# Layer norms of a two-block network: mean, squares, high parts and first tiles rearranged

## The reference

```python
def second_block(x, w_in, conv_w, w_out, ln1_g, ln1_b, w_up, ffn_conv_w, w_down, ln2_g, ln2_b, rel_bias):
    for l in range(DEPTH):                                       # DEPTH = 2
        mix = hybrid_mixer(x, w_in[l], conv_w[l], w_out[l], rel_bias)
        x = layer_norm(DN_ALPHA * x + mix, ln1_g[l], ln1_b[l])   # "norm", l, 0
        f = conv_ffn(x, w_up[l], ffn_conv_w[l], w_down[l])
        x = layer_norm(DN_ALPHA * x + f, ln2_g[l], ln2_b[l])     # "norm", l, 1
    return x

def layer_norm(x, g, b):
    mu = jnp.mean(x, axis=-1, keepdims=True)
    var = jnp.mean(jnp.square(x - mu), axis=-1, keepdims=True)
    return (x - mu) * lax.rsqrt(var + LN_EPS) * g + b

def conv_ffn(h, w_up, ffn_conv_w, w_down):
    u = h @ w_up                                  # 1024 -> 2 x 2816
    a, b = u[..., :D_FF], u[..., D_FF:]
    a = causal_dwconv(a, ffn_conv_w)              # 3 taps
    return (gelu(a) * b) @ w_down                 # 2816 -> 1024
```

## Time and profile before

| | us |
|---|---|
| median of 3 runs | 2670.54 (2667.34 to 2671.54) |
| the profiled execution | 2673.33 |
| its span (first to last instruction) | 2671.5 |
| PE busy | 2513.2 (94%) |
| DVE busy | 1814.5 (68%) |
| ACT busy | 1312.6 (49%) |
| POOL busy | 29.6 (1%) |
| chain that ended last | PE 83%, DVE 9%, ACT 6% |

### The profile page before, as it was taken

How to read it: one execution, slowest core, us unless ns; L and a number is a source line. 1 busy time by engine, 2 the same in 40 slices (tenths; PEclk the granted TensorE clock), 3 DMA queues, 4 the chain that set the end, 5 groups by cost and what they waited for, 6 DMA issues and landing times.

```text
span 2671.5 us, 33651 instructions
## 1 busy us (share of the span) xinstructions
PE 2513.2 (94%) x13358; PEld 2053.7 (77%) x13358; DVE 1814.5 (68%) x2870; ACT 1312.6 (49%) x1981; POOL 29.6 (1%) x29
## 2 busy tenths in 40 slices
PE   6999998999998989899999999999898999998998
PEld 3464657788776658688788887888798899988998
DVE  4778626676431434699899898898867675576774
ACT  2135513222222343577677776787644554444553
POOL 0000000000000000000000000000000000000000
PEclk8999998999998989899999999999999899998999
DMA  7522023555321102498898897898843345432552
GB/s 287 189 109 96 1 79 111 189 203 190 125 79 48 64 32 80 184 353 340 309 366 325 324 368 292 325 366 328 310 143 125 111 174 201 146 128 109 176 188 95
DMA packets 71675, 512.06 MB, mean 192 GB/s; under 512 B 7904, under 2 KB 9056, under 8 KB 10048
## 3 DMA queue, kind: packets, MB, share of 16 engines
q1 hardware_dynamic: 68688, 500.20, 50.2%
q10 hardware_dynamic: 2208, 7.37, 0.7%
q0 software_dynamic: 592, 1.97, 0.2%
HBM read 507.27 MB, written 2.23 MB: 191 GB/s over the span
## 4 chain that ended last, share of the span: by engine, by line
PE 83%; DVE 9%; ACT 6%; issue 1%; DMA 1%; DVEq 0%; ACTq 0%
PE bank L767 81%; DVE UL L1892 1%; ACT UH L1433 1%; DVE arena L1900 1%; DVE arena L1892 1%; ACT arena L1436 1%; ACT HT L1436 1%; DMA XT<-in_x 1%; PE bank L1076 1%; DVE HGl L1892 1%; DVE HT L1892 1%; ACT L1436 1%; DVE JUNK L1939 0%; DVE arena L1896 0%; DVE small L1959 0%
## 5 line engine op out<-in xcount | busy, mean ns | idle before, releaser
L1892 DVE TENSOR_TENSOR UL<-ring,UH 128x1024 fp32r<-128x1024 f32 x738 | 886.0, 1212 | 213.6 <-ACT UH L1433 194.3
L1433 ACT CAST UH<-ring 128x1024 fp32r<-128x1024 f32 x738 | 761.4, 1039 | 352.7 <-PE bank L767 344.5
L767 PE MATMUL bank<-XH,UH 128*128 128x256 f32 x1040 | 308.9, 297 | 9.6 <-DVE XL L1892 8.3
L767 PE MATMUL bank<-UH,HGh 128*128 128x512 f32 (+1 forms) x768 | 292.8, 381 | 17.9 <-DVE HT L1892 6.6
L767 PE MATMUL bank<-XL,UH 128*128 128x256 f32 x1040 | 297.6, 286 | 0.0
L767 PE MATMUL bank<-XH,UL 128*128 128x256 f32 x1040 | 297.3, 286 | 0.0
L767 PE MATMUL bank<-UH,HGl 128*128 128x512 f32 (+1 forms) x768 | 289.9, 377 | 0.0
L767 PE MATMUL bank<-UL,HGh 128*128 128x512 f32 (+1 forms) x768 | 288.9, 376 | 0.0
L1433 ACT CAST UH0a<-ring 128x1024 fp32r<-128x1024 f32 x66 | 69.0, 1048 | 324.1 <-PE bank L767 318.7
L767 PEld LDWEIGHTS bank<-XH,UH 128*128 128x128 f32 x1040 | 201.8, 194 | 22.0 <-issue 15.5
L1939 DVE CUSTOM_DVE_ANT_0 JUNK<-ring,CROW 128x1024 bf16<-128x1024 f32 x176 | 206.0, 1218 | 17.8 <-ACT CROW L1436 17.1
(11 more groups left out here) (210 smaller groups left out, 4380.9 us busy)
## 6 DMA issues: line engine op xcount, KB each, us to landing
ring<-in_w SPq DMA_DIRECT2D x477, 1024.0 KB, 4.8
XT<-in_x ACTq DMA_DIRECT2D x1, 2048.0 KB, 20.2
bias_scratch<-BIAS POOLq DMA_DIRECT2D x6, 192.0 KB, 2.1
consts<-in_c ACTq DMA_DIRECT2D x1, 1109.0 KB, 8.0
CROW<-in_r ACTq DMA_DIRECT2D x1, 1024.0 KB, 13.3
out_y<-XT ACTq DMA_DIRECT2D x2, 512.0 KB, 3.5
BIAS<-bias_scratch POOLq DMA_DIRECT2D x1, 768.0 KB, 7.9
constd<-in_c ACTq DMA_DIRECT2D x1, 768.0 KB, 4.2
```

What stands on the lines that cost most here:

```text
L767: return e.matmul(out, lhsT, rhs, start=start, stop=stop, skip_group_check=True)
L1433: return e.copy(out, in_)
L1892: return e.tensor_tensor(out, a, b, op)
```

## The change

- **The mean.** TensorE's function `mean_part` makes the mean's products of some blocks. In `wo2_end` it is called for the two blocks of the pair before, ahead of each pair but the first, and for the last two at the end; in the down projection for block m-1 behind tile m, and for block 7 at the end. The mean's PSUM bank is taken before the stage's last part.
- **The squares.** GpSimd adds the squared blocks 0 and 1, 2 and 3, 4 and 5. TensorE sums five blocks in place of eight, in the order pair 0, pair 2, block 6, block 7, pair 4.
- **The high part.** ScalarE's ACTIVATE with the shift writes `XH` at once; `X` keeps the unshifted value. VectorE makes `XL` as (X + shift) - XH in one instruction with three operands. GpSimd adds the shift to `X` later (`shifted`), after the low parts; the next evictions into `X` wait for it. The last norm writes `X` from ScalarE as before.
- **The first two tiles.** A new step `duo` replaces the two first `split` steps at each layer's start (mk tiles 0 and 1) and at the up projection's start (u1 and u3 of m = 0): TensorE makes block k's three products for both tiles before it goes on to block k+1. Both units have to be ready before the first product.

```diff
--- before.py
+++ after.py
@@ -224,6 +224,10 @@
         groups = [range(k0, min(k0 + 8, nk)) for k0 in range(0, nk, 8)]
         out.append(("split", name, [((name, k0), key, idx, [(128 * k, c0, 128) for k in ks])
                                     for k0, ks in zip(range(0, nk, 8), groups)]))
+
+    def duo(a, b, key, idx, ca, cb):
+
+        out.append(("duo", (a, b), [((n, 0), key, idx, [(128 * k, c, 128) for k in range(8)]) for n, c in ((a, ca), (b, cb))]))
 
     out.append(("silu",))
     pump(2)
@@ -360,8 +364,10 @@
                 out.append(steps_m.pop(0))
             out.extend(extra)
 
-        for m in range(3):
-            proj2("mk", l, m, c0=1920 + 128 * m)
+        duo(("mk", l, 0), ("mk", l, 1), key, ix, 1920, 2048)
+        out.append(("evict2", ("mk", l, 0)))
+        out.append(("evict2", ("mk", l, 1)))
+        proj2("mk", l, 2, c0=2176)
         for m in range(3):
             proj2("mq", l, m, c0=1536 + 128 * m)
         by_token2("mval", 2304)
@@ -400,8 +406,11 @@
         out.append(("norm", l, 0))
         out.append(("up2", l))
         for m in range(NF):
-            split("u1", l, m, key="w_up_2", idx=ix, c0=128 * m)
-            split("u3", l, m, key="w_up_2", idx=ix, c0=FF + 128 * m)
+            if m == 0:
+                duo(("u1", l, 0), ("u3", l, 0), "w_up_2", ix, 0, FF)
+            else:
+                split("u1", l, m, key="w_up_2", idx=ix, c0=128 * m)
+                split("u3", l, m, key="w_up_2", idx=ix, c0=FF + 128 * m)
             out.append(("gate2", l, m))
         for m in range(8):
             split("d2", l, m, key="w_down_2", idx=ix, c0=128 * m, nk=NF)
@@ -466,7 +475,7 @@
         self.last = [len(self.last) - self.last[::-1].index(s) for s in self.last]
 
 
-SPLITS = ("split", "rows2", "wo2", "f2", "up", "down")
+SPLITS = ("split", "duo", "rows2", "wo2", "f2", "up", "down")
 
 
 def build(nc, np_cols, nc_cols):
@@ -1192,21 +1201,24 @@
                 else:
                     i.then_inc(*sums.up(("wo2", l, pair), *([("unit", u) for u, _, _ in us] if pair == 3 else [])))
 
+            def mean_part(l, n, ks):
+
+                for k in ks:
+                    w.wait_ge(*vec.at("wo2" if n == 0 else "d2", l, k))
+                    op = mm(psum(("mean", l, n))[:, 0:256], con("M1024"), X[:, k, xs], k == 0, k == 7)
+                if ks[-1] == 7:
+                    op.then_inc(*sums.up(("mean", l, n)))
+                    give(("mean", l, n))
+
             def norm(l, n):
-                prev = "wo2" if n == 0 else "d2"
-                b = take(w, ("mean", l, n))
-                for k in range(8):
-                    w.wait_ge(*vec.at(prev, l, k))
-                    op = mm(b[:, 0:256], con("M1024"), X[:, k, xs], k == 0, k == 7)
-                op.then_inc(*sums.up(("mean", l, n)))
-                give(("mean", l, n))
-                b = take(w, ("var", l, n))
-                for k in range(8):
-                    w.wait_ge(*act.at("var", l, n, k))
+                tile = ("var", l, n)
+                b = take(w, tile)
+                for at, k in enumerate((0, 2, 6, 7, 4)):
+                    w.wait_ge(*(act.at("var", l, n, k) if k > 5 else pool.at("pair", l, n, k)))
                     for t in range(2):
-                        op = mm(b[:, t:t + 1], H[:, k, 128 * t:128 * t + 128], con("one", 0, 1), k == 0 and t == 0, k == 7)
-                op.then_inc(*sums.up(("var", l, n)))
-                give(("var", l, n))
+                        op = mm(b[:, t:t + 1], H[:, k, 128 * t:128 * t + 128], con("one", 0, 1), at == 0 and t == 0, at == 4)
+                op.then_inc(*sums.up(tile))
+                give(tile)
                 spread_root(("var", l, n), 2)
 
             w.wait_ge(s_load[0], 16)
@@ -1281,12 +1293,36 @@
                     if at < 5:
                         w.wait_ge(*vec.at("cl", l, k))
                         out_block(l, range(8), (k,))
+                elif kind == "duo":
+                    what, l = st[1][0][0], st[1][0][1]
+                    if what == "u1":
+                        b = take(w, ("u", l, 0))
+                        dsts, part = (b[:, 0:256], b[:, 256:512]), "mid"
+                    else:
+                        dsts, part = [take(w, n_)[:, 0:256] for n_ in st[1]], "in"
+                    us = [unit(p[0]) for p in st[2]]
+                    for u, _, _ in us:
+                        w.wait_ge(*lo_ready.at(u))
+                    for k in range(8):
+                        w.wait_ge(*vec.at("xl", l, part, k))
+                        c = slice(128 * k, 128 * k + 128)
+                        for n_, (u, wh, wl) in enumerate(us):
+                            mm(dsts[n_], wh[:, c], XH[:, k, :], k == 0 and (what != "u1" or n_ == 0), False)
+                            mm(dsts[n_], wh[:, c], XL[:, k, :], False, False)
+                            i = mm(dsts[n_], wl[:, c], XH[:, k, :], False, k == 7)
+                            if k == 7:
+                                i.then_inc(*sums.up(("unit", u), st[1][n_]))
+                    give(*([("u", l, 0)] if what == "u1" else st[1]))
                 elif kind == "wo2_end":
+                    take(w, ("mean", l, 0))
                     for p in range(4):
+                        if p:
+                            mean_part(l, 0, (2 * p - 2, 2 * p - 1))
                         for k in CAT_ORDER[5:]:
                             w.wait_ge(*vec.at("cl", l, k))
                         out_block(l, (2 * p, 2 * p + 1), CAT_ORDER[5:], p)
                         give(("wo2", l, p))
+                    mean_part(l, 0, (6, 7))
                 elif kind == "vm":
                     _, l, part, tb = st
                     tile = ("vm", l, part, tb)
@@ -1335,11 +1371,17 @@
                                   lambda k: vec.at("xl", l, "mid", k))
                         give(("u", l, m))
                     elif what == "d2":
-                        l = st[1][1]
+                        l, m = st[1][1], st[1][2]
+                        if m == 0:
+                            take(w, ("mean", l, 1))
                         b = take(w, st[1])
                         by_halves(st, st[1], b[:, 0:256], lambda k: Gh2[:, k, :], lambda k: Gl2[:, k, :],
                                   lambda k: vec.at("gl2", l, k))
                         give(st[1])
+                        if m:
+                            mean_part(l, 1, (m - 1,))
+                        if m == 7:
+                            mean_part(l, 1, (7,))
                     else:
                         l = st[1][1]
                         b = take(w, st[1])
@@ -1666,11 +1708,8 @@
                 nxt = (l, "mid") if n == 0 else (l + 1, "in")
                 for k in range(8):
                     w.wait_ge(*vec.at("scaled", l, n, k))
-                    apply(X[:, k, xs], X[:, k, xs], ACT.Identity,
-                          bias=par(f"l{n + 1}b{l}", k)).then_inc(*act.up(("normed", l, n, k)))
-                    if not end:
-                        w.wait_ge(*act.now())
-                        copy(XH[:, k, :], X[:, k, xs]).then_inc(*act.up(("xh",) + nxt + (k,)))
+                    apply(X[:, k, xs] if end else XH[:, k, :], X[:, k, xs], ACT.Identity, bias=par(f"l{n + 1}b{l}", k)).then_inc(
+                        *act.up(("normed", l, n, k) if end else ("xh",) + nxt + (k,)))
 
             def load(i, dst, src):
                 e.dma_start(dst, src).then_inc(s_load[i], 16)
@@ -1768,6 +1807,8 @@
                     modulated("n2", 0, 3, "n2g", 0, True)
                 elif kind == "split":
                     split_high(unit(st[2][-1][0])[0], UNITS + 1 if st[1][0] in ("f1", "f3") else UNITS)
+                elif kind == "duo":
+                    split_high(unit(st[2][-1][0])[0], UNITS)
                 elif kind == "rows2":
                     split_high(unit(st[2][-1][0])[0], UNITS)
                     what, l = st[1]
@@ -2356,7 +2397,10 @@
                         stt(X[:, k, xs], X[:, k, xs], par(f"l{n + 1}g{l}", k), psum(wide)[:, 0:256], ALU.mult,
                             ALU.mult).then_inc(*vec.up(("scaled", l, n, k), free=[wide]))
                     if k >= 2 and not end:
-                        low_parts(nxt, k - 2)
+                        j = k - 2
+                        w.wait_ge(*act.at("xh", *nxt, j))
+                        stt(XL[:, j, :], X[:, j, xs], par(f"l{n + 1}b{l}", j), XH[:, j, :].bitcast(F32), ALU.add,
+                            ALU.subtract).then_inc(*vec.up(("xl",) + nxt + (j,)))
                 if not end:
                     split_low(W.first["ahead", l, n], UNITS)
 
@@ -2516,6 +2560,7 @@
                         tt(ZC[:, m, 2:258], CC[:, m, :], b[:, 0:256], ALU.mult).then_inc(*vec.up(tile, free=[tile]))
                     elif what == "d2":
                         w.wait_ge(*sums.at(*tile))
+                        w.wait_ge(*pool.at("normed", l, 0, m))
```

(23 more changed lines are left out.)

## The result

The changed kernel takes 2683.7 us, median of five runs (2683.3 to 2685.9), against 2671.5 (2667.3 to 2674.9): ratio 1.0047, 95% interval 1.0032 to 1.0061, so 12.2 us slower. I had forecast +6.4 us and 2669.5 to 2682.5. The sign was right, the size about half of what came; the median lies 1.2 us above the range.

The account below looks back on a forecast made before the run. The chain of waits was taken as almost wholly TensorE, with the up projection bound by the loop feeding it. Terms +9.6 - 1.6 - 3.6 + 2.0 = +6.4 us on 2670.5 gave 2676.9; range 2673 to 2680, with rivals 2669.5 to 2682.5.

Parts of the forecast that it names:

- (a): Mean's products among the last sums: +4.6 us per norm behind output projection (eviction waits), +0.2 behind down projection; sum +9.6.
- (b): Variance's products at the norms, 20 instead of 32 with GpSimd adding pairs: -0.4 us each, -1.6 in all.
- one held up: Upper bound for the variance's squares: GpSimd additions at 1.06 us each, one of them delayed, +0.5 us a norm.
- (c): High part straight from the shift, one ScalarE operation per block; together with (d) -3.6 us, bounds -6.5 and -0.5.
- (d): First two tiles block by block: -0.9 and -2.1 us at the layer starts, -0.3 at each of two up projections.
- w: Time from the two tiles' start until TensorE's clock rises: between 2.3 and 5.8 us, middle 4.1.
- (e): GpSimd's 24 added shifts in three places, off the path but possibly holding VectorE up: +1.0 us in all.
- 1 (clock kept up from the start of the tiles): Interleaved products keep TensorE at full clock in the first two tiles: 2669.7 us, not slower; chance 0.10.
- 2: Mean's waits for evictions aren't paid, each gap under 0.2 us: 6.0 us less, 2670.9; chance 0.05.
- 3: GpSimd blocks VectorE at layer 1's start, up projections and last pair's addition: 4 to 5 us more, 2681; chance 0.15.
- 4: Up projection keeps the gain of the first tiles, fourth unit's cast being hidden: -1.6 us twice, 2673.7; chance 0.05.

Follow-up runs that it names:

- (a) alone: The kernel before with only the mean's products moved among the last sums: 2686.9 us, ratio 1.006 (1.0043 to 1.0077).
- the order turned: Kernel with high parts and first tiles, at the up projection's start the fourth unit cast behind ScalarE's copy, its low part behind the convolution: ratio 0.999, -2.7 us.

## Why the prediction was half right

Laid beside the table: for the mean I had 10.6 us (9.6 and 1.0 for the clock), 10.9 came. For the variance stretch I had -1.6, +3.9 came. For the shift, the first tiles and what GpSimd does beside them I had -2.6, -2.1 came. So 5.5 of the about 6 us that I missed lie between the first square and the reading of the variance.

**What bounds the kernel** held: each shift at a norm went through to the end, and the up projection passed on little of what its start gained.

**(a), the mean at n = 0: right, and the largest term.** Three gaps a layer between the pairs and one behind them, 0.78 us of record behind evictions of 0.69, mean pieces of 1.13; the casts then hold the squares. Worked out +4.6 and up to 1.5 for a prolonged half clock. In the traces +4.4 in layer 1, and +6.0 in layer 0, where the half clock indeed lasted to 2077. That the sum of both came out so near has luck in it: the first gap met a half clock in one layer and not in the other. **At n = 1** +0.2 and +0.2, as worked out.

**(a), what it does behind itself: the missing term.** I ended the working of (a) at the first square. The mean's block of 3.61 us was also what kept TensorE dense right ahead of the variance. With it spread out, the variance's products fell into half clock: 6.1 us on average over the four norms of the mean alone, 4.9 over twenty norms of five kernels in which the mean's block and all 32 products stand as before, among them the 4.6 of the profile that I read. Filling products brought it back to 4.5. That is 1.2 to 1.6 us at each of four norms, 5 to 6 us, and with it (a) alone comes to +13 to +16 in place of +9.6. The clock's fall at the variance is in the profile before too (TensorE at 0.50 from inside the first norm on); I weighed it for the output projection and the two tiles only.

**(b), the squares: the step that failed.** It said "the last twelve instructions (blocks 6, 7 and the last pair) at 0.128 take 1.54 from 2.5 on: end 4.1", for -1.6 us in all. The trace shows +3.9. Three sizes make it up. The addition takes 0.72 us; I took 0.6, no matter. But the products don't start before 1.6 us, they come late and with waits between them, and the granted clock is 0.50 for about the last twelve (for all twenty at the first norm): 0.214 each, 2.57 us. I had priced them at full clock. And at n = 0 the third addition was held to 1.70 us by the low part, the "one held up" of my upper bound. Measured alone, (b) is +1.5 us (-1.1 to +4.3), and without the additions about 0. On top of (a), whose clock is low anyway, 20 products are even shorter than 32 (5.6 us on average against 6.1). So which of the two edits the +3.9 belongs to can't be said: either alone lengthens the variance stretch as much as both together (5.6 us for the squares alone, 6.1 for the mean alone, 5.6 for both), and the profile of before, with 4.6, had it shorter than the 4.9 of the twenty norms.

**(c) and (d): right in kind, up to 1.5 us too good.** Their -3.6 stands against -2.1, in which what the shifts cost is already contained. The first product came 1.80 behind the first scaling, as said. The working of the two tiles can be followed here:

```profile
2099.02 7.95 PE bank L776 x45
...
2107.05 1.05 ACT UH L1475
```

The chain counts the 45 products up to the end of the first tile; the last three of the second follow. They come without a gap, and the clock rises 5.3 us behind the first: 5.76 + 0.44 x 5.3 = 8.1, and 1.8 + 8.1 = 9.9 behind the scaling. The formula held; my middle of 4.1 us for w did not hold in this profile. It was 5.6, 5.3, 5.1 and 3.6 at the four places, hardly earlier than before (5.6, 5.2, 6.3 and 4.8), though TensorE was full. But it differs between executions: in the kernel with the first tiles alone it was 3.9 to 4.4, and with high parts and first tiles 6.1 once and 3.0 to 3.1 three times, where the tiles ended 8.9 to 9.0 us behind the scaling. In the up projection:

```profile
2108.12 1.22 DVE L1933 TENSOR_TENSOR UL<-ring,UH 128x1024 fp32r<-128x1024 f32 x1 [3.39 <-ACT UH L1475]
2109.27 0.57 DVE L1937 TENSOR_SCALAR CV<-CV,params 128x256 f32<-128x256 f32 x1
```

```profile
2107.05 1.05 ACT L1475 CAST UH<-ring 128x1024 fp32r<-128x1024 f32 x1 [4.09 <-PE bank L776]
...
2112.22 1.99 ACT L1475 CAST UH<-ring 128x1024 fp32r<-128x1024 f32 x2
```

The convolution starts 2.1 behind the second tile (2.2 forecast), TensorE waits 1.5 us ahead of its fifth unit (1.3 forecast), the loop takes back what the tiles won: +0.4 and -0.4 against -0.3 each.

**(e) Both inputs of VectorE from SBUF beside GpSimd.** A GpSimd addition and a VectorE subtraction with two SBUF inputs held each other up, 1.22 to 1.80 us and 0.72 to 1.79 us. By the rule of the Trainium skill, SBUF — State Buffer, section "Who interferes with whom", that such a pair excludes each other, one of the two should wait and the other keep its time; the additions of the experiments agree. The shifts at layer 1's start don't. They took 0.9 us there (1.09 on average, where I had priced 0.5), and stretched the low parts only a little (0.48, then 0.54 and 0.59):

```profile
2310.20 0.48 DVE L1941 SCALAR_TENSOR_TENSOR XL<-XT,params,XH 128x256 fp32r<-128x256 f32 x1
...
2310.98 0.54 DVE L1941 SCALAR_TENSOR_TENSOR XL<-XT,params,XH 128x256 fp32r<-128x256 f32 x1
...
2311.84 0.59 DVE L1941 SCALAR_TENSOR_TENSOR XL<-XT,params,XH 128x256 fp32r<-128x256 f32 x1
```

```profile
2310.77 1.83 POOL L2662 TENSOR_SCALAR XT<-XT,params 128x256 f32<-128x256 f32 x2 [2.52 <-DVE XL L1941]
```

The low part at 2310.98 began inside the first shift, which ran to about 2311.7, and was done by 2311.52: it didn't wait for the shift's end. The stretching cost no time that I could separate, since the clock set the two tiles' pace.

**The rivals.** 1 (clock kept up from the start of the tiles) happened nowhere in the changed kernel's profile; helped by filling products it is the fastest one. 2 is out: the waits are in the trace. 3 is right as a mechanism for the additions; with a third addition about 1 us longer at two norms and the stretched low parts it is too small to be the cause. 4 is out: the loop took the gain; half of the convolution's delay comes back with the order turned, in layer 1.

**What stays open.** How much of the +12.2 is the chain and how much the clock can be said only to about 3 us: single parts add up to 1.0059 by their ratios against 1.0047 for the whole, and where the clock's changes fall differs from one execution to the next. The same 32 products took 3.6 to 6.4 us. One profile of each kernel is one draw.

## What to carry to other kernels

Before a block of work is spread out of a serial stretch, ask what it covered there: here it hid an eviction, and it kept TensorE's clock up for what followed. A product placed directly behind the sums that feed its operand, through another engine, waited the eviction's whole length here every time; one group later it didn't wait at all. In a latency-bound stretch at half clock, products that compute nothing can be worth more than removing real ones, as long as they fit into the wait. And where the clock changes from one execution to the next, a single profile prices such a stretch at one draw: the 4.6 us that I started from were 4.9 over twenty norms.

## What the runs showed of the hardware that I had not expected

- One-column float32 products come 0.112 us apart at full clock and 0.214 at half; so they are no cheaper than 256-column ones of rounded operands (fp32r: 0.120 and 0.213), and the clock fell while they ran in most norms.
- A GpSimd addition of two 128x256 float32 blocks takes 0.72 us alone and up to 1.79 when a VectorE instruction with two SBUF inputs is under way; this one takes 1.80 in place of 1.22 when GpSimd is first.
- VectorE's 128x256 multiply by a scalar took 0.57 us in place of 0.35 while GpSimd added shifts in one kernel, and between 0.35 and 0.57 in the others; a low part beside a shift of 0.9 us grew only from 0.48 to 0.54 to 0.59.
- Filling products alone, with no edit of the work, gave 0.9986 (0.9976 to 0.9995).
